# Squared-ReLU MLP of a two-layer trunk: weight sums on VectorE, refills on ScalarE's queue, and a reordered opening

## The reference, cut to what matters

```python
for i in range(2):
    hn = rms_norm(h, mix_norm[i])
    h = h + mixer_i(hn) @ w_out_i
    hn = rms_norm(h, mlp_norm[i])
    h = h + jnp.square(jax.nn.relu(hn @ w_mlp_in[i])) @ w_mlp_out[i]   # 1024 -> 4096 -> 1024
    hn = rms_norm(h, ple_norm[i])
    h = h + (p[i] @ w_ple_up[i]) * jax.nn.sigmoid(hn @ w_ple_gate[i])
return rms_norm(h, final_norm)
```

## Time and profile before

| | us |
|---|---|
| median of 3 runs | 2492.68 (2490.14 to 2494.17) |
| the profiled execution's own time | 2494.89 |
| its span | 2493.2 |
| TensorE busy, share of the span | 2314.5, 93% |
| VectorE | 1642.3, 66% |
| GpSimd | 1092.2, 44% |
| ScalarE | 939.2, 38% |
| mean granted clock of TensorE | 0.966 of full |
| HBM traffic over the span | 110 GB/s |

### The profile page before, as it was taken

The page is one execution under the profiler, slowest core; times in us unless marked ns, Lnnn a source line. Parts: engine busy times, 40 slices in busy tenths (PEclk is TensorE's granted clock), DMA queues, the critical chain, the costliest instruction groups (busy, mean ns, idle before and its releaser), DMA issues.

```text
span 2493.2 us, 31423 instructions
## 1 busy us (share of the span) xinstructions
PE 2314.5 (93%) x12286; PEld 1860.1 (75%) x12286; DVE 1642.3 (66%) x1917; ACT 939.2 (38%) x1470; POOL 1092.2 (44%) x686
## 2 busy tenths in 40 slices
PE   8998967998999889999998999988899979999997
PEld 6887846786888768887786776666788868887786
DVE  6868279558677677668627355657767776768825
ACT  3120155443333344433312245645333343334315
POOL 4433212145555455555332343645445554565421
PEclk9998978998999999999999999998999999999998
DMA  7372432212343644542113111121334465335111
GB/s 211 101 124 63 120 120 62 94 42 93 127 172 133 211 160 164 174 168 69 51 51 101 34 34 51 45 58 34 152 127 165 153 227 190 118 132 167 41 51 68
DMA packets 226084, 277.86 MB, mean 111 GB/s; under 512 B 33572, under 2 KB 172040, under 8 KB 221832
## 3 DMA queue, kind: packets, MB, share of 16 engines
q1 hardware_dynamic: 212392, 257.14, 31.5%
q10 hardware_dynamic: 13552, 18.81, 2.9%
HBM read 190.53 MB, written 84.21 MB: 110 GB/s over the span
## 4 chain that ended last, share of the span: by engine, by line
PE 64%; DVE 18%; issue 5%; ACT 5%; DMA 4%; POOL 2%; ACTq 1%; SPq 0%; DVEq 0%; POOLq 0%
PE ps L1202 32%; PE ps L831 15%; PE ps L1368 3%; PE ps L982 2%; DMA st_raw<-w_mlp_out_in 2%; PE ps L1400 2%; DVE st_lo L2447 2%; DVE mid_sums L2483 2%; DVE mid_last_sum L2489 1%; ACT quads L1451 1%; PE ps L1328 1%; POOL st_lo L670 1%; DVE quads L2478 1%; DVE stage L1953 1%; DVE hg_queries_keys L2291 1%
## 5 line engine op out<-in xcount | busy, mean ns | idle before, releaser
L1202 PE MATMUL ps<-op,st_hi 128*128 128x512 f32 x3584 | 1128.7, 397 | 74.3 <-ACT quads L1451 31.7
L1202 PEld LDWEIGHTS ps<-op,st_hi 128*128 128x128 f32 x3584 | 682.5, 191 | 233.4 <-issue 61.7
L1202 PE MATMUL ps<-op,st_lo 128*128 128x512 f32 x1792 | 706.7, 394 | 0.0
L670 POOL TENSOR_TENSOR st_lo<-st_raw,st_hi 128x512 fp32r<-128x512 f32 x192 | 306.0, 1596 | 525.6 <-ACT st_hi L1451 524.8
L1202 PEld LDWEIGHTS ps<-op,st_lo 128*128 128x128 f32 x1792 | 342.2, 191 | 73.1
L633 POOL CAST w_hi<-w_raw 128x1024 fp32r<-128x1024 f32 x66 | 74.6, 1131 | 482.4 <-issue 251.5
L1451 ACT ACTIVATE st_hi<-st_sum 128x512 fp32r<-128x512 f32 x256 | 159.0, 628 | 301.4 <-POOL st_sum L664 164.0
L1451 ACT ACTIVATE st_hi<-st_raw 128x512 fp32r<-128x512 f32 x192 | 121.0, 631 | 365.9 <-PE ps L1202 145.5
L2447 DVE TENSOR_TENSOR st_lo<-st_sum,st_hi 128x512 fp32r<-128x512 f32 x256 | 230.7, 910 | 10.9 <-ACT st_hi L1451 9.5
L2510 DVE TENSOR_TENSOR residual<-residual,ps 128x512 f32<-128x512 f32 x192 | 130.9, 682 | 116.7 <-PE ps L1202 116.3
L2518 DVE TENSOR_TENSOR op<-op_raw,op 128x1024 fp32r<-128x1024 f32 x112 | 175.6, 1568 | 39.4 <-ACT op L1451 39.4
(11 more groups left out here) (339 smaller groups left out, 3540.4 us busy)
## 6 DMA issues: line engine op xcount, KB each, us to landing
op_raw<-mid_dram SPq DMA_DIRECT2D x56, 1024.0 KB, 5.2
st_raw<-w_mlp_in_in SPq DMA_DIRECT2D x32, 1024.0 KB, 5.7
mid_dram<-quads SPq DMA_DIRECT2D x32, 1024.0 KB, 3.9
st_raw<-w_mlp_out_in SPq DMA_DIRECT2D x32, 1024.0 KB, 5.9
mid_dram<-mid_sums SPq DMA_DIRECT2D x32, 512.0 KB, 3.5
w_raw<-w_in_even_in SPq DMA_DIRECT2D x20, 512.0 KB, 4.5
residual_dram<-residual ACTq DMA_DIRECT2D x2, 4096.0 KB, 12.8
mid_dram<-mid_last_sum SPq DMA_DIRECT2D x32, 256.0 KB, 2.4
```

Of the source, the lines that this page charges most:

```text
L670: pool.tensor_tensor(SL[r][:, :, :], x, SH[r][:, :, :].bitcast(F32), sub).then_inc(S["st_lo_pool"], 1)
L1202: ins = pe.matmul(PS[:, o, :], w[:, j, :], OP[s][:, x, j, :], start=(s < 3 and j == 0 and w is SH[r] and x == 0), stop=(j == 3 and w is SL ...
```

## The change

- The four weight sums of a job are made by VectorE: `first_sums` at places 12 and 13 of the set before, `last_sums` at places 2 and 3 of its own (the first and last sets of an MLP have places of their own). GpSimd keeps the lows of products 0, 3 and 6 alone.
- VectorE makes all mid sums of the first job at place 2, the first and second of the second job at place 3, its last at place 5 as before.
- `x_operands` is cut into three steps, and the steps of neighbouring tiles interleaved: residual of m, lows of m - 1, difference of m.
- `late_operand` moves from GpSimd into VectorE's `late_last`, which comes earlier. ScalarE's `copy(1, 0)` stands ahead of `cast_late(4)`, and `cast_late(6)` comes earlier.
- The 28 refills of an MLP move from SyncE's queue to ScalarE's, issued three products before their cast.
- The z additions of the last block become three of 128 x 512, at products 3, 4 and 5, and in the last set one of the last two tiles is reported ready after product 5.
- Raw loads wait for VectorE's sums too.

```diff
-                    if k >= SETS // 2 and k % 2 == 0 and r == 0 and k < SETS - 1:
-                        refill((k - SETS // 2) // 2, 6)
-                    if k >= SETS // 2 - 1 and k % 2 and r and r % 2 == 0 and k < SETS - 1:
-                        refill((k - SETS // 2 + 1) // 2, r // 2 - 1)
...
                         sp.wait_ge(S["st_lo_pool"], low_pool(i, g + b, 6))
+                        sp.wait_ge(S["st_sum"], summed(i, g + b, 5))
                         raw(g + 2 + b)
...
-                for k in range(SETS - 1):
-                    for g in (2 * k, 2 * k + 1):
-                        first_sum(g)
-                        low(g, 0)
-                        second_sum(g)
...
+                for g, s in LOW_POOL:
+                    low(g, s)
...
+                def refill(c, s):
+                    act.wait_ge(S["st_prod"], made(i, UP - 1 + 4 * c, s))
+                    if s == 0:
+                        for b in range(2):
+                            act.wait_ge(*set_stored(i, 4 * c + 2 + b))
+                            act.wait_ge(mt_stored[b], 16 * (UP // 2 * i + 2 * c + 2))
+                        act.wait_ge(S["t4_stored"], 16 * (UP * i + 4 * c + 4))
...
                 copy(0, 0)
+                copy(1, 0)
                 cast_late(i, 4, 9, 9)
                 high(8)
-                copy(1, 0)
                 cast_late(i, 5, 9, 9)
                 high(9)
+                cast_late(i, 6, 10, 11)
                 high(10)
                 copy(0, 3)
                 high(11)
                 copy(1, 3)
-                cast_late(i, 6, 10, 11)
                 high(12)
                 high(13)
                 for t in range(10, PRODUCTS + 1):
...
+                    kj, rj = divmod(t - 2, 2 * SLOTS)
+                    if kj >= SETS // 2 - 1 and kj % 2 and kj < SETS - 1 and rj % 2 == 0:
+                        refill((kj - SETS // 2 + 1) // 2, rj // 2)
...
-                def x_operands(m):
-                    j = m // 2
+                def x_residual(m):
                     dve.wait_ge(S["acc_done"], u0 + m + 1)
                     tt(H[:, m, :], flat(first if m == 0 else ACC[m % 2]), H[:, m, :], add).then_inc(S["acc_free"], 1)
                     dve.wait_ge(S["acc_free"], free_of(u0)[1] + m)
                     dve.nop().then_inc(S["h_ready"], 1)
+
+                def x_sum(m):
+                    j = m // 2
                     dve.wait_ge(S["op_x_scaled"], X_SCALED * i + m + 1)
                     if m % 2 == 0:
                         tt(OPF[2][:, 1, j, :], OPF[2][:, 1, j, :], OPF[0][:, 1, j, :], sub).then_inc(S["op_x_sum"], 1)
-                        dve.wait_ge(S["op_cast"], cb + 2 * m + 1)
-                        tt(OP[0][:, 1, j, :], OPF[0][:, 1, j, :], OP[0][:, 0, j, :].bitcast(F32), sub).then_inc(S["op_ready"], 1)
                     else:
                         dve.wait_ge(S["op_x_sum"], X_SUMS * i + m)
                         tt(OPF[1][:, 1, j, :], OPF[1][:, 1, j, :], OPF[2][:, 1, j, :], sub).then_inc(S["op_x_sum"], 1)
+
+                def x_lows(m):
+                    j = m // 2
+                    dve.wait_ge(S["op_cast"], cb + 2 * m + 1)
+                    if m % 2 == 0:
+                        tt(OP[0][:, 1, j, :], OPF[0][:, 1, j, :], OP[0][:, 0, j, :].bitcast(F32), sub).then_inc(S["op_ready"], 1)
+                    else:
                         dve.wait_ge(S["op_x_sum"], X_SUMS * i + m + 1)
-                        dve.wait_ge(S["op_cast"], cb + 2 * m + 1)
                         tt(OP[1][:, 1, j, :], OPF[1][:, 1, j, :], OP[1][:, 0, j, :].bitcast(F32), sub).then_inc(S["op_ready"], 1)
...
                 def late_last():
+                    dve.wait_ge(S["op_x_scaled"], X_SCALED * i + 10)
+                    dve.wait_ge(S["op_ready"], rb + 12)
+                    tt(OPF[6][:, 1, :, :], OPF[6][:, 1, :, :], OP[1][:, 0, :, :].bitcast(F32), sub).then_inc(S["op_x_sum"], 1)
                     dve.wait_ge(S["op_x_sum"], X_SUMS * i + 10)
                     tt(OPF[6][:, 1, :, :], OPF[6][:, 1, :, :], OP[1][:, 1, :, :].bitcast(F32), sub).then_inc(S["op_x_sum"], 1)
                     dve.wait_ge(S["op_x_sum"], X_SUMS * i + 11)
+
+                def first_sums(g):
+                    dve.wait_ge(yt_raw_loaded[raw_of(g)], raw_visit(i, g))
+                    if g >= 2:
+                        dve.wait_ge(S["st_lo"], low_dve(i, g - 2, 5))
+                    elif i:
+                        dve.wait_ge(S["st_lo"], low_dve(i - 1, JOBS - 1, 5))
+                    tt(sum_of(g, 2), quarter(g, 1, 0), quarter(g, 1, 1), add).then_inc(S["st_sum"], 1)
+                    dve.wait_ge(S["st_sum"], summed(i, g, 2))
+                    tt(sum_of(g, 1), sum_of(g, 2), quarter(g, 0, 0), sub).then_inc(S["st_sum"], 1)
+
+                def last_sums(g):
+                    dve.wait_ge(S["st_lo"], low_dve(i, g, 2))
+                    tt(sum_of(g, 4), quarter(g, 0, 0), quarter(g, 1, 0), sub).then_inc(S["st_sum"], 1)
+                    tt(sum_of(g, 5), quarter(g, 0, 1), sum_of(g, 1), sub).then_inc(S["st_sum"], 1)
...
-                        if c == 3:
-                            dve.wait_ge(S["st_ev"], ev(i, g, 0))
-                            right = H[:, 2 * q:2 * q + 2, rights]
-                            tt(right, right, Z1[q][:, :].unsqueeze(1).to_broadcast([P, 2, HALF]), add)
-                            own(tt(h21, h21, z, add))
...
+                    if c == 3 and s in (3, 4, 5):
+                        h = (h12, h21, h22)[s - 3]
+                        if s != 4:
+                            dve.wait_ge(S["st_ev"], ev(i, g, s // 4 * 3 + 1))
+                        own(tt(h, h, z, add))
+                    if c == 3 and s == 5 and g // 2 == SETS - 1:
+                        dve.wait_ge(S["st_ev"], ev(i, g, 5))
+                        dve.nop().then_inc(S["h_ready"], 1)
+                    if c == 3 and s == 6:
                         dve.wait_ge(S["st_ev"], ev(i, g, 6))
-                        for _ in range(2):
+                        for _ in range(1 if g // 2 == SETS - 1 else 2):
...
                 start_norm()
-                for m in range(7):
-                    x_operands(m)
+                x_residual(0)
+                x_sum(0)
+                for m in range(1, KT):
+                    x_residual(m)
+                    x_lows(m - 1)
+                    x_sum(m)
+                    if m >= KT - 2:
+                        first_sums(m - KT + 2)
                 weight_low(2)
-                x_operands(7)
+                x_lows(KT - 1)
                 weight_low(3)
                 end_norm()
                 weight_low(4)
                 weight_low(5)
+                last_sums(0)
+                last_sums(1)
                 late_difference()
+                late_last()
                 block_low(4, 17)
                 for s in (1, 2):
...
                     if t > UP * SLOTS and product_at(t - 1) not in COPIES:
                         evict_down(*product_at(t - 1))
+                    if k < SETS - 2 and r >= 12 or k == SETS - 2 and r == 12:
+                        first_sums(g + 2 + r - 12)
+                    if k == SETS - 1 and r == 4:
+                        first_sums(g + 1)
                     if t + 3 < PRODUCTS:
                         weight_low(t + 3)
+                    if 1 <= k < SETS - 1 and r in (2, 3):
+                        last_sums(g + r - 2)
+                    if k == SETS - 1 and r in (0, 7):
+                        last_sums(g + r // 7)
                     if k < SETS // 2 and r == 13:
                         scaled(g)
                     if 1 <= k <= SETS // 2:
@@ -2584,11 +2586,10 @@
                             scaled(g - 1)
                         if r == 2:
                             first_mid_sums(g - 2)
+                            second_mid_sum(g - 2)
+                            last_mid_sum(g - 2)
                         if r == 3:
                             first_mid_sums(g - 1)
-                            second_mid_sum(g - 2)
-                            last_mid_sum(g - 2)
-                        if r == 4:
                             second_mid_sum(g - 1)
                         if r == 5:
                             last_mid_sum(g - 1)
```

55 lines of the change are left out of this document (6 added, 49 removed).

## The result

| | before | changed |
|---|---|---|
| median | 2491.59 (2490.14 to 2494.17, 4 runs) | 2524.52 (2515.20 to 2529.05, 4 runs) |
| profiled execution | 2494.89 | 2515.20 |
| TensorE, mean granted clock | 0.966 | 0.964 |

The ratio is 1.0129, 95% interval 1.0102 to 1.0155: the changed kernel is slower, by 33 us. The forecast had the sign, and its range (2447 to 2525) just holds the median, but it said +14.5.

The account below looks back on a forecast made before the run. TensorE, 93% busy, was taken as bound by whichever wait ends last before it in each stage. Terms -28.1 + 53 + 6 - 13.4 - 3 = +14.5 gave 2509.4, or 2507 us as median; range 2447 to 2525.

Parts of the forecast that it names:

- the place where the change is paid for and the chain of it: Steady sets 3 to 7: late squares delay the last sum, ScalarE's copy and the eighth product; +53 us.
- All three named rivals: GpSimd gets no turn, 2452, chance 0.20; last sum not held by squares' store, 2447, 0.13; VectorE becomes the bound, 2525, 0.10.
- Set 15: Z additions spread over three evictions no longer block VectorE, so nothing is lost there or in set 13; -13.4 us.
- the opening: Start of each MLP: -5.8 us in layer 0 and -22.3 in layer 1, together -28.1.
- 12.5, so 0.0 and -2.6: From eighth product through set 2: late low and waits cost 12.5 us, so 0.0 in layer 0, -2.6 in layer 1.
- at 1690.2: -13.7: Layer 1's opening: the fifth product ends at 1690.2 instead of 1703.9, 13.7 us sooner.
- With the three steps interleaved, a tile costs VectorE ... 4.2 in the mean: Layer 1's opening: VectorE needs 4.2 us a tile, under the unit's 5.44, and its waits are filled.
- At the end one tile is ready a product sooner: End of the MLP: TensorE's wait of 1.09 us and some slow clock are saved; -3 us for both layers.
- Here it is paid back: Steady sets: VectorE's chain to the second job's subtractions grows from 13.6 to 18.1 us; 5.3 a set, +53 in all.
- the first rival: Steady sets: GpSimd gets no turn, except where VectorE waits for its own result; +10 there, 2452 us in all, chance 0.20.
- The eighth product's gain: MLP's first set: moving ScalarE's bank copy ahead of a waiting cast frees 6.7 us in layer 0, 6.0 in layer 1.
- the refills' move: 28 issues per MLP go to ScalarE; waits in sets 8 and 9 grow by the stores' shift, +6 us for both MLPs.

Follow-up runs that it names:

- second trace: The changed kernel run once more, unaltered, for another trace; median 2523.59 us, ratio 1.0122 to the kernel before, profiled execution 2525.2.
- Experiment 2: Changed kernel with the first job's mid sums and last sum stored ahead of the second job's squares on SyncE's queue; 2452.62 us, ratio 0.9835.
- experiments 5 to 7: Changed kernel with weight sums back on GpSimd (2517.54 us), with the old order of the mid sums (2462.17), and with both (2450.48).
- experiment 9: Changed kernel with sums stored before squares and later last weight sums (2430.46 us), plus copy(1, 0) put back behind cast_late(4); 2433.48 us.
- experiment 10: Changed kernel with sums stored before squares and later last weight sums (2430.46 us), plus refills back on SyncE's queue; 2446.28 us.
- experiment 5: Changed kernel with the four weight sums given back to GpSimd, the new order of the mid sums kept; 2517.54 us, ratio 1.0091.

## Why the prediction was right and wrong

By its own terms, forecast beside measured (second trace of the changed kernel against the profiled execution before, which differ by 30.3). An opening is counted from VectorE's first addition to the residual:

| term | forecast | measured |
|---|---|---|
| opening to the fifth product of the MLP, layer 0 | +0.9 | +1.7 |
| the same, layer 1 | -13.7 | -11.6 |
| eighth product, both | -12.7 | -12.8 |
| from there through set 2, layer 0 | 0.0 | +5.9 |
| the same, layer 1 | -2.6 | +0.8 |
| sets 3 to 7, both | +53 | +50.7 |
| sets 8 and 9 | +6 | +6.7 |
| set 15 (and 13) | -13.4 | -13.4 |
| end of the MLP | -3 | -0.9 |
| start of the gate behind it, both | in the -3 | +2.5 |

The remaining 0.7 is the sum of small differences ahead of the first opening (-0.9), in layer 1's mixer (+1.2) and at the end (+0.6).

**Right:** the place where the change is paid for and the chain of it, each of its points within 0.2 us: squares at 15.3, last sum landed at 21.1, product at 22.8. All three named rivals are refuted by these traces: GpSimd got its turns, the last sum was held, and sets 10 to 14, which have most of the refills' lows, take 38.1 each. Experiment 2 adds that the same load runs 72 us faster. Set 15 was right to 0.1: its products take 5.44 again.

**Wrong in size: the opening.** It was to give 28.1 and gave 16.0, in the first trace too, and these 12 us are most of the 16 that the sum missed. The step that failed most is "12.5, so 0.0 and -2.6": 9.3 us. It costed late weight lows at one place in set 2 alone and none in the first set. The changed kernel (first trace) has them at four products, three of them in the first set:

```profile
566.75 0.74 PE L1147 MATMUL ps<-op,st_hi 128*128 128x512 f32 x2 [0.86 <-DVE st_lo L2429]
...
572.98 0.73 PE L1147 MATMUL ps<-op,st_hi 128*128 128x512 f32 x2 [0.45 <-DVE st_lo L2429]
...
576.87 0.72 PE L1147 MATMUL ps<-op,st_hi 128*128 128x512 f32 x2 [0.88 <-DVE st_lo L2429]
...
597.00 1.22 PE L1147 MATMUL ps<-op,st_hi 128*128 128x512 f32 x2 [3.18 <-DVE st_lo L2429]
```

The first three are 3.1 us lost in each layer (by the products' ends); the fourth is 3.2 of wait and the slow clock behind it, 6.0 and 4.9 together where the forecast had 1.9. VectorE's last sums, `late_last` and the root stand ahead of these lows in its program; no run takes them out one by one. The other two waits of set 2 were forecast at 10.6 and took 9.4 and 8.8 in the second trace.

The second step is the sum that ends "at 1690.2: -13.7". From its first residual VectorE reaches the eighth tile after 39.5 us (forecast 38.8), and from there to the end of the fifth product it takes 17.9 (forecast 16.4): 2.1 us more together. "With the three steps interleaved, a tile costs VectorE ... 4.2 in the mean" is wrong too, but without a price. It took a low at 0.6, and GpSimd splits the projection's weights at that time (VectorE, second trace):

```profile
1663.36 2.83 DVE L2383 TENSOR_TENSOR op<-op_raw,op 128x512 fp32r<-128x512 f32 x1
...
1674.44 2.66 DVE L2383 TENSOR_TENSOR op<-op_raw,op 128x512 fp32r<-128x512 f32 x1
...
1689.19 1.22 DVE L2366 TENSOR_TENSOR residual<-ps,residual 128x1024 f32<-128x1024 f32 x1 [1.28 <-PE ps L776]
```

Two such meetings cost 4.1 on VectorE, but at the seventh tile it waits for TensorE again, so they are made good by then.

**Wrong in sign: the end of the MLP.** "At the end one tile is ready a product sooner" was to give 3 us. In the MLP it gave 0.9, but TensorE waits 1.6 to 1.7 us for a low in the gate's first unit where it waited 1.1, and 0.3 once more, and behind these waits the gate is 1.2 to 1.3 us later than before, in both layers and in every trace of the changed kernel and its variants. In the changed kernel a z addition (L2492, 2.3 us) stands ahead of these lows on VectorE. That it is the cause is read from the order, no run puts it back.

**Right in number, not in every part.** "Here it is paid back", said of the moved work as a whole, was a sum over 16 operations, four scalings and the two mid sums of the first job; these two were put in at 1.4, with 2.2 more for two GpSimd lows somewhere in the stretch. In the trace the two take 3.3, since each waits for VectorE's own result and lets GpSimd in, as the first rival's text says. So the price was right, and the six moved weight sums at 0.60 stand in the same sum with as much, 3.6. What the sum does not say is which of the two can be spared. The square of experiments 5 to 7 does: the mid sums' order is worth 62 to 67 us, the weight sums' place 7 to 12, since on GpSimd they stretch VectorE's operations instead. 0.4 us of wait and 3.75 lie 3.4 us of VectorE apart. The eighth product's gain was put down to the moved copy, and the copy does nothing (experiment 9): that number was right by luck. And the refills' move was costed at nothing beside the stores' shift; the shift is there, but once the order is right the move is worth 16 us (experiment 10).

**Turns and queues.** A lone low of GpSimd takes 1.29 us; beside VectorE in set 6 of the changed kernel a pair took 6.13:

```profile
772.85 6.13 POOL L639 TENSOR_TENSOR st_lo<-st_raw,st_hi 128x512 fp32r<-128x512 f32 x2 [9.15 <-ACT st_hi L1396]
```

It got in only where VectorE waited for its own result; with GpSimd's sums in a row (experiment 5) the two alternate. The Trainium skill ("SBUF — State Buffer", on who interferes with whom) describes a lock held for a whole instruction, and the rows agree; what decides the next turn stays open. Of the queues experiment 10 and its neighbours show a store that lands after 8.5 to 9.1 us behind a refill, from the same queue or from another, and after 5.5 ahead of it. The Trainium skill ("DMA: Bandwidth & Descriptors", rules for kernel authors) says that issuing from more engines brings no bandwidth, since all transfers run on the same DMA engines; these numbers agree. But the prediction took it as a reason to price the move at nothing, and here it was worth 16 us through the moment at which the refill goes out.

**Open.** Why the move of the weight sums costs 12 us with the old order was not taken apart; by the traces 9 of it stand in sets 3 to 7, of which 6 in two sets alone, and 3 in sets 8 and 9. Why layer 1's mixer is 1.2 us longer in the second trace than before is open too. Whether the sums on GpSimd would come to 2425 with an order made for them wasn't tried.

## What to carry to other kernels

When a store is on the path, the order of its queue has to follow the order in which an in-order engine makes the data, and a small early transfer must not stand behind a large late one; changing either order alone moved this kernel by 14 to 72 us, and in both directions. Moving a transfer to another engine's queue changes when it goes out, since it then waits for what that engine waits for; look at whether it passes the one on the path. An instruction that reads the result of the one just before it is dearer than its duration says when another engine waits for the port, so it should not stand ahead of what others wait for. And a term that comes out right is no proof of its cause: undo the part alone before keeping it.

## What the runs showed of the hardware

A 1 MB store took 9.1 us to land when a 1 MB refill had been issued 2.1 us ahead of it on the same queue, 8.5 with the refill 1.5 us ahead on another engine's queue, and 5.5 when the refill came 1.5 us after it. GpSimd's lows took 6.1 and 7.2 us a pair beside VectorE's back-to-back operations. A wait of 3.5 to 4.0 us was followed by the lower clock in 16 of the 20 eighth products of sets 3 to 7 in the two traces, and this is half of the 10 us between them; executions of the changed kernel spread over 14 us where those before spread over 4.
